# The first expert's tokens picked on chip by one-hot products in a float32 encoder trunk

## The reference

```python
logits = (t @ router_w).astype(F32) + router_b.astype(F32)
probs = jax.nn.softmax(logits, axis=-1)
grouped = probs.reshape(-1, N_GROUPS, EXPERTS_PER_GROUP)
group_score = jnp.sum(lax.top_k(grouped, TOP_K)[0], axis=-1)
g_sel = jnp.argmax(group_score, axis=-1)
...
top_v, top_i = lax.top_k(jnp.where(in_group, probs, -1.0), TOP_K)
gates = top_v / jnp.sum(top_v, axis=-1, keepdims=True)
combine = jnp.sum(jax.nn.one_hot(top_i, N_EXPERTS, dtype=F32) * gates[..., None], axis=1)
for e in range(N_EXPERTS):
    gu = t @ w_gu[e]
    h = jax.nn.silu(gu[:, :D_EXPERT]) * gu[:, D_EXPERT:]
    out = out + combine[:, e:e + 1] * (h @ w_down[e]).astype(F32)
```

## Time and profile before

| | |
|---|---|
| three runs | 877.88, 884.35, 884.72 us |
| profiled execution | 882.92 us |
| its span, from the first instruction to the last | 881.1 us |
| TensorE busy | 855.2 us, 97% of the span |
| VectorE, ScalarE, GpSimd busy | 568.4, 428.1, 128.8 us |
| mean granted TensorE clock | 0.986 |

### The profile page before, as it was taken

One profiled execution on the slowest core, in us unless ns is written; L12 is line 12 of the kernel. 1 busy time (PEld: TensorE's weight loads), 2 busy tenths in 40 slices (PEclk: granted clock), 3 DMA queues, 4 the chain that ended last, 5 costly groups with the idle time before them and its releaser, 6 DMA issues.

```text
span 881.1 us, 9990 instructions
## 1 busy us (share of the span) xinstructions
PE 855.2 (97%) x4004; PEld 685.7 (78%) x4004; DVE 568.4 (65%) x716; ACT 428.1 (49%) x429; POOL 128.8 (15%) x126
## 2 busy tenths in 40 slices
PE   8999999999899999999998999999999999999986
PEld 5888888888778678888874888888887678888843
DVE  4532434456565789999976625425666699999937
ACT  4433222443422378888874131122214288888850
POOL 3400000020400114325220000000000223233110
PEclk9999999999999999999999999999999999999988
DMA  9983313112439299999969522230256699999862
GB/s 348 361 325 96 96 48 96 48 49 96 144 143 373 85 366 349 364 354 341 342 231 380 193 96 96 95 96 1 96 212 265 199 394 345 358 332 343 312 234 96
DMA packets 80834, 193.84 MB, mean 220 GB/s; under 512 B 8249, under 2 KB 8437, under 8 KB 80656
## 3 DMA queue, kind: packets, MB, share of 16 engines
q1 hardware_dynamic: 67344, 159.46, 50.3%
q0 software_dynamic: 13440, 33.69, 10.4%
HBM read 178.95 MB, written 30.43 MB: 238 GB/s over the span
## 4 chain that ended last, share of the span: by engine, by line
PE 91%; DVE 4%; ACT 2%; DMA 2%; issue 1%; POOL 0%; SPq 0%; POOLq 0%; ACTq 0%
PE ps L495 62%; PE ps L852 9%; PE ps L572 4%; PE ps L555 3%; PE ps L795 3%; PE ps L622 2%; PE ps L607 2%; PE ps L710 2%; PE ps L823 1%; DMA expert_out<-arena,rows_of 1%; DVE w_lo L1352 1%; PE ps L581 1%; DVE xt_lo L1360 1%; PE ps L703 1%; DVE xt_lo L1789 1%
## 5 line engine op out<-in xcount | busy, mean ns | idle before, releaser
L1352 DVE TENSOR_TENSOR w_lo<-arena,w_hi 128x2048 fp32r<-128x2048 f32 x100 | 229.5, 2297 | 128.2 <-ACT w_hi L1036 126.7
L1036 ACT ACTIVATE w_hi<-arena 128x2048 fp32r<-128x2048 f32 x100 | 191.5, 1915 | 158.6 <-PE ps L495 150.5
L495 PE MATMUL ps<-w_hi,xt_hi 128*128 128x512 f32 x480 | 192.8, 402 | 0.0
L495 PE MATMUL ps<-w_hi,xt_lo 128*128 128x512 f32 x480 | 188.1, 392 | 0.0
L495 PE MATMUL ps<-w_lo,xt_hi 128*128 128x512 f32 x480 | 187.8, 391 | 0.0
L495 PE MATMUL ps<-xt_hi,w_hi 128*128 128x512 f32 (+1 forms) x352 | 131.9, 375 | 1.9 <-DVE xt_lo L1360 1.9
L495 PE MATMUL ps<-xt_hi,w_lo 128*128 128x512 f32 (+1 forms) x352 | 130.3, 370 | 0.0
L495 PE MATMUL ps<-xt_lo,w_hi 128*128 128x512 f32 (+1 forms) x352 | 130.1, 370 | 0.0
L495 PEld LDWEIGHTS ps<-w_hi,xt_lo 128*128 128x128 f32 x480 | 90.5, 189 | 19.2
L495 PEld LDWEIGHTS ps<-w_lo,xt_hi 128*128 128x128 f32 x480 | 90.6, 189 | 17.8
L495 PEld LDWEIGHTS ps<-w_hi,xt_hi 128*128 128x128 f32 x480 | 90.5, 189 | 17.6
(11 more groups left out here) (239 smaller groups left out, 998.4 us busy)
## 6 DMA issues: line engine op xcount, KB each, us to landing
arena<-in_moe_w_gu SPq DMA_DIRECT2D x64, 1024.0 KB, 16.7
arena<-in_moe_w_down SPq DMA_DIRECT2D x32, 1024.0 KB, 17.8
arena<-in_mlstm_w_in SPq DMA_DIRECT2D x16, 1024.0 KB, 7.1
arena<-in_conv_w_in SPq DMA_DIRECT2D x12, 1024.0 KB, 12.1
expert_out<-ln_b POOLq DMA_DIRECT2D x8, 1024.0 KB, 13.7
arena<-expert_out SPq DMA_DIRECT2D x16, 512.0 KB, 7.8
arena<-in_mlstm_w_out SPq DMA_DIRECT2D x4, 1024.0 KB, 5.0
x_of_experts<-arena SPq DMA_DIRECT2D x8, 512.0 KB, 10.3
```

The source lines that it names most:

```text
L495: ins = pe.matmul(out, a, b, start=first and n == 0, stop=last and n == 2)
L1036: act.activation(w_hi[:, parity, :], raw(slot), ACT.Copy).then_inc(s_hi, 1)
L1352: dve.tensor_tensor(w_lo[:, parity, :], raw(slot), w_hi[:, parity, :].bitcast(F32), ALU.subtract).then_inc(s_lo, 1)
```

## The change

Expert 0 no longer gathers from DRAM. VectorE makes four more one-hot tiles, of expert 0 alone (token against place), and TensorE multiplies the four normed tiles `zn`, still on chip, with them. The result is the transposed token tile itself, in two halves of 512 features (banks 0 and 1), each by 16 float32 products. The hi and lo parts are made by halves as well. The spins between the routing steps go, and two of the six ahead of them. Four small operations of `choose` that only the gates need are moved behind the choice, the computation of the gates behind the start of the expert loop, and their product (`slot_gates`) behind the first expert's products. POOL's first gathers are now of expert 1 and 2, and SP's held loads wait for the end of the second half and for the gather of expert 1.

```diff
@@ SP, expert_loads
-                            sp.wait_ge(s_gat[0], 16 * (E // 2) * layer + 16)
+                            sp.wait_ge(s_gtr, E * layer + 1)
+                            sp.wait_ge(s_gat[1], 16 * (E // 2) * layer + 16)
@@ TensorE, out_projection, router
-                spin(6, 5)
+                spin(4, 5)
...
-                spin(1, 5)
+                first_tokens(layer, 0)
                 for n in range(2 * NT):
                     pe.wait_ge(s_oh, 2 * NT * layer + n + 1)
                     ins = slot_table(values, 0, n)
                 ins.then_inc(s_ixm, 1)
-                spin(2, 5)
+                first_tokens(layer, 1).then_inc(s_gtr, 1)
+
+            def first_tokens(layer, half):
+
+                for t in range(NT):
+                    if half == 0:
+                        wait_x(pe, 2 * layer, t)
+                        pe.wait_ge(s_foh, NT * layer + t + 1)
+                for c in range(4 * half, 4 * half + 4):
+                    for t in range(NT):
+                        ins = pe.matmul(ps[:, half, (c % 4) * P:(c % 4 + 1) * P], zn[:, t, c * P:(c + 1) * P],
+                                        first_hot[:, t, :], start=t == 0, stop=t == NT - 1)
+                if half == 0:
+                    ins.then_inc(s_fx, 1)
+                return ins
+
+            def slot_gates(layer):
                 pe.wait_ge(s_gv, layer + 1)
                 for n in range(2 * NT):
                     ins = slot_table(gates, 1, n)
                 ins.then_inc(s_gm, 1)
-                spin(4, 5)
@@ TensorE, experts
-                tokens_T(0, 0)
-                spin(1, 5)
                 gate_up_half(0, 0)
+                gate_up_half(0, 1)
                 tokens_T(1, 1)
-                gate_up_half(0, 1)
+                slot_gates(layer)
@@ ScalarE, experts
-                gathered_hi(0, 0)
+                first_hi(0)
+                first_hi(1)
@@ VectorE, choose
+                per_expert = r_rank.rearrange("p k (t e) -> p k t e", t=NT)
+                do(dve.tensor_tensor(first_place[:, :], per_expert[:, 0, :, 0], per_expert[:, 1, :, 0], ALU.add))
+                for t in range(NT):
+                    dve.tensor_scalar(first_hot[:, t, :], place_no[:, :], first_place[:, t:t + 1], None,
+                                      ALU.is_equal).then_inc(s_foh, 1)
                 do(dve.tensor_reduce(place[:, :, :].rearrange("p k t -> p (k t)"),
@@ VectorE, experts
-                dve.wait_ge(s_gi, layer + 1)
                 units(0, 0, 0)
+                first_lo(0)
+                first_lo(1)
                 units(0, 0, 1)
-                gathered_lo(0, 0)
+                shares_by_expert()
                 units(1, 1, 0)
                 gathered_lo(1, 1)
+                slot_gates(layer)
                 hidden(0, 0)
@@ POOL, experts
-                for e in range(2):
+                for e in range(1, 3):
                     gather(e, e)
-                pool.engine_nop().then_inc(s_gi, 1)
                 norm_weights(1 + 2 * layer, ln2_g[layer], ln2_b[layer])
-                for e in range(2, 4):
-                    gather(e, e)
+                gather(3, 3)
```

More of the change, by code:

```diff
@@ L287, in trunk @@
         s_oh = sem("one_hot_ready")
+        s_fx = sem("first_half_gathered")
+        s_foh = sem("first_one_hot_ready")
         s_ixm = sem("rows_multiplied")
@@ L789, in tokens_T @@
                 def tokens_T(e, j):
-                    pe.wait_ge(s_gat[j % 2], 16 * ((E // 2) * layer) + gathers(e, j))
-                    if e >= 1:
-                        pe.wait_ge(s_glo, e + c0)
+                    pe.wait_ge(s_gat[j % 2], gathers(e, j))
+                    pe.wait_ge(s_glo, 2 * (e + c0))
                     for c in range(KC):
@@ L827, in gate_up_half @@
                     four(xe_hi, w_hi, True, False)
[L828 to L831, removed]
+                    if e == 0 and kh == 1:
+                        pe.wait_ge(s_glo, 2 * (e + c0) + (kh + 1))
+                        four(xe_lo, w_hi, False, False)
+                        pe.wait_ge(s_lo, e * 2 + (SPLIT0[layer] + kh + 1))
+                        four(xe_hi, w_lo, False, True).then_inc(s_hl, 1)
+                    else:
+                        pe.wait_ge(s_lo, e * 2 + (SPLIT0[layer] + kh + 1))
+                        four(xe_hi, w_lo, False, False)
+                        pe.wait_ge(s_glo, 2 * (e + c0) + (kh + 1))
+                        four(xe_lo, w_hi, False, True).then_inc(s_hl, 1)
                 def hidden_T(e, j):
@@ L864, in gathers @@
                 def gathers(e, j):
-                    return (e - (j % 2)) * 8 + 16
+                    return 16 * (E // 2) * layer + e * 8 + 8 if e % 2 else 16 * (E // 2 - 1) * layer + e * 8
                 def step(e, j, turn, left):
@@ L1186, in experts, with first_hi @@
                 c0 = E * layer
+                def first_hi(half):
+                    if half == 0:
+                        act.wait_ge(s_fx, layer + 1)
+                    else:
+                        act.wait_ge(s_gtr, c0 + 1)
+                    act.activation(xe_hi[:, 0, 4 * half:4 * half + 4, :],
+                                   ps[:, half, :].rearrange("p (c s) -> p c s", c=4), ACT.Copy).then_inc(s_ghi, 1)
                 def gathered_hi(e, j):
@@ L1719, in choose @@
                 step_done(dve.tensor_reduce(r_most, groups(r_key), AX.X, ALU.max))
[L1720 to L1723, removed]
+                step_done.wait()
                 step_done(dve.tensor_tensor(groups(r_tops[:, 1, :]), groups(r_key), wide(r_most, GE), ALU.is_equal))
[L1725 to L1731, removed]
+                step_done.wait()
+                step_done(dve.tensor_tensor(
+                    top[:, :, :, :].rearrange("p k t (g e) -> p k (t g) e", e=GE),
+                    r_tops.rearrange("p k (g e) -> p k g e", e=GE),
+                    r_group.unsqueeze(1).unsqueeze(3).to_broadcast([P, 2, NT * NG, GE]), ALU.mult))
                 step_done.wait()
@@ L1735, in choose @@
                 step_done(by_expert(values, facts))
+                step_done(dve.tensor_tensor(r_gated[:, 0, :], r_first, r_group, ALU.mult))
+                step_done(dve.tensor_tensor(r_gated[:, 1, :], r_second, r_group, ALU.mult))
+                step_done.wait()
+                step_done(dve.tensor_reduce(top_value[:, :, :].rearrange("p k t -> p (k t)"),
+                                            r_gated.rearrange("p k (t g) -> p (k t) g", t=NT), AX.X, ALU.add))
                 dve.wait_ge(s_rank, layer + 1)
```

19 lines of the change are left out of this document (13 added, 6 removed).

## The result

The change made the kernel slower. Six runs of the changed kernel have a median of 887.13 us (884.86 to 890.87), six of the kernel before 883.36; the ratio is 1.0077 [1.0042, 1.0113]. A second set, next to other experiments, gave 1.0111 [1.0057, 1.0165]. The forecast was 881.5 in a range of 877.5 to 886.0.

The account below looks back on a forecast made before the run. TensorE, busy 97%, and the weight transfers were both taken to bound expert stages; the change shortens the seam's chain. 882.92 us less 0 in layer 0 and 1.4 in layer 1 gave 881.5, range 877.5 to 886.0.

Parts of the forecast that it names:

- The 1.0 that VectorE was said to take back of the 2.4: First experts: expert 0 starts 2.4 us earlier, VectorE's later row numbers and lo parts leave 1.4 of it per layer.
- The lead of the first held load: SP's first held weight load landing ahead of its reader: near 10 us, not 13.5.
- Layer 0 has 1.6 at expert 14: 2.1 short: Layer 0, expert 14's down weights: lead 1.6 shrinks by 3.7; ScalarE's 0.59 wait leaves 1.5 stall, gain taken as 0.
- Layer 1 has 3.2: 0.5 short, which the same wait covers, so it keeps 1.4: Layer 1, expert 14's down weights: lead 3.2 shrinks by 3.7, ScalarE's 0.59 wait covers the shortfall, 1.4 us gained.
- an upper bound (884.1): Weight stream delayed 3.6 us by norm weights' later issue: lead shrinks 5.0, layer 0 1.4 longer, layer 1 0.2 shorter.
- the rule of 3.2 us: POOL's gather by the skill's rule, 3.2 us not 4.3: stream only 1.2 late, layer 0 keeps its gain, 880.1.
- half of 1.8 above 884.3: Range's upper end: outcomes reach 884.3, plus half the 1.8 us by which earlier runs lay above the profiled one.
- The clock falls ahead of the first half: Rival, new products' first half at half rate: 1.4 us more, 3.55 at most, total 884.3; chance 0.28.
- Both gains stay: Rival, expert stages: the weight stream catches up, both layers keep 1.4 us, total 880.1; chance 0.20.
- late gather: Rival, expert 1's gather takes twice 4.3 us: TensorE waits 0.7, the stream is 4.3 later, total 890; chance 0.06.
- dear products: Rival, new products cost 0.216 us a record like wide ones: each half 3.35 us longer, total 893; chance 0.04.

Follow-up runs that it names:

- the lo part elsewhere: Changed kernel with VectorE's first lo part of weights moved ahead of its wait for the row numbers: 881.57 us, 1.0004 to the kernel before.
- the norm weights early: Changed kernel with POOL issuing the two norm-weight loads (1 MB) between its first and second gathers: 881.55 us, 1.0008 to the kernel before.
- the spin's run: Changed kernel with one spin pass put back between the places' product and the first new product: 887.03 us, 1.0058 to the kernel before.
- lo part and norm weights early: Changed kernel with first lo part ahead of the row numbers and norm weights between POOL's first two gathers: 880.57 us, 0.9986.
- lo part, norm weights and spin: Changed kernel with first lo part before row numbers, norm weights between POOL's first two gathers, one spin pass before the new products: 878.24 us, 0.9959.

## Why the prediction was wrong

**What held.** The first product (299.9 forecast, 299.76 measured), 0.11 us a record, expert 0 at 308.0 (307.79), row numbers at 304.5 (304.41), the hidden tiles of expert 0 and 1 at 317.3 and 326.5 (317.24 and 326.10). The 1.0 that VectorE was said to take back of the 2.4 came as 0.9 of 2.8, though from TensorE's gates and ScalarE's hi part, so that this size agrees by luck. The lead of the first held load, 13.5 before, was forecast near 10 and is 9.7. Layer 0 stalls, and the copies wait for transfers, as said.

**The step that failed.** "Layer 0 has 1.6 at expert 14: 2.1 short", and "Layer 1 has 3.2: 0.5 short, which the same wait covers, so it keeps 1.4". They take the delay of the first held load, 3.7 us, off the lead at expert 14 as it is. But the lead does not keep its distance: in layer 0 it is 3.9 less at expert 3, 5.6 at expert 7 and 6.5 at expert 9's down weights; in layer 1, 4.7, 5.3 and 7.6. Expert 9's down weights in layer 0, before and then after (issue, time to landing, ScalarE's copy):

```profile
372.03 5.72 SPq L356 DMA_DIRECT2D arena<-in_moe_w_down  x1
DMA to landing us min/median/max: 20.3/20.3/20.3
402.53 1.92 ACT L1209 ACTIVATE xt_hi<-arena 128x2048 fp32r<-128x2048 f32 x1 [0.59 <-PE ps L852]
...
376.33 4.40 SPq L359 DMA_DIRECT2D arena<-in_moe_w_down  x1
DMA to landing us min/median/max: 20.7/20.7/20.7
400.76 1.92 ACT L1240 ACTIVATE xt_hi<-arena 128x2048 fp32r<-128x2048 f32 x1 [0.59 <-PE ps L876]
```

The lead is 10.2 before and 3.7 after. The waits start at expert 12 and not at 14, and are 2.2 and 4.5 us, where 1.5 and nothing was forecast. Nor was expert 14 the tightest place before: expert 15's down weights landed 0.3 us ahead of their copy in layer 0 and 2.9 in layer 1, so that even the same subtraction would have come out 3.4 and 0.8 short there.

**What was left out of the sum.** VectorE's wait for POOL's first gathers was removed, and the text followed only what it did for VectorE. That wait had kept the lo part off the gather: without it the issue takes 2.37 us, and the held loads start 1.3 later than forecast. Taken alone it decides: with the lo part elsewhere the loss is gone. The trace of before held a sign of it in POOL's third gather, which ran beside the second lo part of the earlier trace rows (to 310.22) and took 1.55 us where the next, without one at its start, took 1.01:

```profile
309.58 1.55 POOL L2030 DMA_INDIRECT arena<-x_of_experts,rows_of  x1 [2.76 <-PE ps L795]
314.60 1.01 POOL L2030 DMA_INDIRECT arena<-x_of_experts,rows_of  x1 [3.46 <-PE ps L795]
```

The norm weights' later issue was taken as an upper bound (884.1), not as part of the forecast; with the norm weights early the loss is gone too. Each of these lets the fifth load land 2.0 to 2.6 us earlier, and either is enough, since the changed kernel lies just past the edge.

**Two sums and a reading in the prediction.** By its own working the rule of 3.2 us leaves layer 0 short by 1.0, of which the wait of 0.59 covers part, so its sum is 880.5 and not 880.1. And half of 1.8 above 884.3 is 885.2, where the range ends at 886.0. The measured 887.13 lies above both ends. The clock of before came back in the third spin of layer 0 and not in the fourth: it reads 0.52 from 295 to 296 us and 1.00 from there on, and the fourth starts at 296.24.

**The rivals.** "The clock falls ahead of the first half" came true in layer 1 at nearly its price: 5.36 for 3.81, 1.55 us for the 1.4 forecast. It fell there in nine of ten profiles of kernels with these products, in layer 0 in two. But by the spin's run it is not what the loss hangs on. With one more spin ahead the clock was still at 0.50 there in two of three profiles; so the rule weighed in the prediction, that activity releases the throttle (the Trainium skill, TensorE: Matmul & The Clock Gate, Part 1), is neither borne out nor refuted at this place. "Both gains stay" did not come in the changed kernel; in the one with lo part and norm weights early no copy waits, as that rival has it. The late gather and the dear products did not come.

**What stays open.** Why the lead shrinks by another 2 to 3 us between experts 3 and 9, and so why the edge is so steep. In the changed kernel the transfers run at 220 and 214 GB/s from 362 to 366 us with four to five loads under way, and such a gap lies in the run of before too (249 GB/s from 350 to 354 us). Why the run with lo part, norm weights and spin is 2.4 us under the one without the spin (by the ratios) is open too: its clock in layer 1's first half was no better, and the intervals overlap.

## What to carry over

A lead of transfers over compute is no account from which a delay is taken off once: look for the first copy that would wait, not only for one small lead at the end, and count everything that is transferred beside it, small loads and gathers too. Before a wait goes out, ask which two things it kept apart, on engines that the wait does not name. And where a stage is near such an edge, moving 1 MB into a stretch in which nothing is transferred can be worth more than a shorter chain.

## What was not expected of the hardware

VectorE's lo part of weights, which has two inputs in SBUF, holds back POOL's issue of an indirect gather, and not its issue of a plain load. More of POOL in layer 0 after the change, two loads of norm weights and two gathers:

```profile
309.33 0.59 POOL L2057 DMA_DIRECT2D ln_g<-in_ln_g  x1
309.91 0.57 POOL L2058 DMA_DIRECT2D ln_b<-in_ln_b  x1
314.65 1.42 POOL L2079 DMA_INDIRECT arena<-x_of_experts,rows_of  x1 [4.17 <-PE ps L813]
319.94 3.05 POOL L2079 DMA_INDIRECT arena<-x_of_experts,rows_of  x1 [3.87 <-PE ps L813]
```

The gather at 305.46 and these two end 0.97, 0.92 and 0.89 us behind the lo part that runs beside them (to 306.86, 315.15 and 322.10); the one at 308.31, with no such part beside it until its end, takes 1.01. The two loads run wholly beside a lo part (309.31 to 311.60) and take 0.59 and 0.57 us, as they do without one (0.57 and 0.57 in layer 1 of the run with the norm weights early). The Trainium skill (SBUF — State Buffer, section on who interferes with whom) says that a VectorE instruction with two SBUF inputs contends with a GpSimd instruction that reads SBUF, and that the order of issue decides who blocks; the trace agrees, with 2.37 us against 1.05, if the gather, whose row numbers lie in SBUF, counts as such a reader, which no run here tests by itself. Only one direction is seen: in layer 1 of the run with the norm weights early a lo part starts 0.12 us behind a gather (699.72 and 699.60), and both take their usual time, 2.28 and 1.04 us. The same section infers that such a tensor_tensor does not stall the writing of a DMA's descriptors; the plain loads agree with that, and the gather's issue is held all the same.
